# A streaming-encoder step on one core: the last four column groups of its input projection in two pairs, each by seven products in place of eight

## The chip, the core and the metric

The kernel runs on one core of one Trainium2 chip. A core has a matrix engine (TensorE, PE in the rows), a vector engine (VectorE, DVE), an activation engine (ScalarE, ACT), GpSimd (POOL) and SyncE (SP), which issues the DMAs. Each engine works through its own queue in order, and semaphores tie the queues together. The metric is the device time of one execution, in microseconds (us).

## The reference

Two layers of an encoder, for 512 new frames of one stream and 16 new frames of each of 8 running streams: 640 rows in all, in five tiles of 128 rows (the fifth is that of the running streams). All weights are shared by the five tiles. What matters here is the input projection, which feeds all three attention branches:

```python
h = _rms(x, p['norm_mix'])
(fq, fk, fv, fg, bq, bk, bv, iq, ik, iw, cqa, ckva, ckpe) = jnp.split(
    h @ p['w_in'], _split_points(IN_SPLITS), axis=-1)
fq = _rms(fq.reshape(B, T, FOX_HEADS, FOX_DIM), p['fox_gq'])   # likewise fk
bq = _rms(bq.reshape(B, T, DSA_HEADS, DSA_DIM), p['dsa_gq'])   # likewise bk, ik
...
g = jax.nn.sigmoid((h @ p['w_gate']).astype(f32)).astype(x.dtype)
x = x + (ga * ya + gb * yb + gc * yc) @ p['w_o']
h2 = _rms(x, p['norm_ffn'])
gt, up = jnp.split(h2 @ p['w_ffn_in'], 2, axis=-1)
x = x + (jax.nn.silu(gt) * up) @ p['w_ffn_out']
```

`h` is 640 x 1024 and `w_in` is 1024 x 2254, in float32.

## The kernel before

**The projection.** The 2254 columns of `w_in` are cut into six groups of 296 to 416 columns (`GROUPS`, L56). A group has four chunks: 256 of the 1024 rows of `w_in` (the contraction) by the group's columns, laid out as 128 partitions by twice the width. The stage with the chunks of group 2 to group 5 is what the change touches: 0 to 384 and 384 to 768 (queries and keys of branch A), 768 to 1158 (its values and gates), 1838 to 2254 (branch C). Groups 0 and 1 (branch B) stand ahead of them, and the gate projection (L872) behind them.

**Split products.** Each float32 operand is split into a high part and a rest, and a product is three matmuls: high by high, high by rest, rest by high. For every chunk ScalarE copies the raw weights into `w_hi` (`hi`, L1362; the instruction itself is L1358 in `copy`), and VectorE subtracts, `w_lo` = raw - `w_hi` (`lo`, L1855 to L1859). There are two buffers of each. `hi(c)` waits until the matmuls of chunk c-2 have ended (`w_used`), and the matmuls of chunk c wait for `lo(c)` (`lo_made`). `h` lies on the chip as `h_hi` and `h_lo`.

**TensorE.** `row_chunk` and `row_part` (L828 to L850): per chunk five tiles, two blocks of 128 contraction rows, three matmuls, so 30 matmuls of one column group's width. The tile of `h` is the stationary operand. Each tile has its own of the eight PSUM banks over the four chunks of a group; after the last chunk ScalarE copies the five results out (`p_d`, `p_i`, `p_qk`, `p_v`, `p_m`), and `proj_out` tells that a bank is free.

**VectorE beside it.** Between two splits `lo` it works on one tile of a branch: `dsa_sums` and `dsa_norm` for branch B in the chunks of groups 2 and 3, `fox_sums` and `fox_norm` for the queries and keys of branch A in groups 4 and 5. "Sums" squares the rows and adds them up per head (`sq_a`, `ssq`, L1927, L1939, L1933). GpSimd turns the sums into inverse roots (`rsq` = power -1/2, L1806), and "norm" multiplies the rows by them. All three queues are in program order: VectorE's is lo(c), norm(t-1), sums(t), lo(c+1), and so on.

**GpSimd.** Ahead of the inverse roots it fills three tiles with zeros (`wz`, `zi`, `lfr`), and beyond them it has nothing to do in this stage. In the feed-forward stage of the same layer it adds and subtracts blocks of weights (`w_sums`, L1829 to L1836), since that stage is already computed by a seven-product scheme.

**SyncE.** `chunk` (L558 to L562) loads each chunk of weights into one of two `raw` buffers, when `lo` has read the one before it.

## Time and profile before

| | us |
|---|---|
| median of three runs | 2193.6 (2193.42 to 2195.47) |
| the profiled execution, its time | 2195.58 |
| the profiled execution, its span | 2193.8 |
| TensorE busy in the span | 2133.1 (97%) |
| VectorE, ScalarE, GpSimd busy | 1378.5, 981.2, 389.4 |
| the four column groups, layer 0 | 59.1 to 145.3 |
| the four column groups, layer 1 | 1146.1 to 1232.3 |

The span is the time from the first to the last instruction of the profiled execution; 1.8 us of its time lie outside it. A busy share says how much of the span an engine worked, not that it set the end: for that the chain of waits is read, which follows the last instruction back to whatever released it. Matmuls overlap, so the duration in a matmul's row is longer than its share of the time; the distance between two starts, or a stretch divided by its matmuls, gives what one costs. The numbers of this table that are not in the page's head come from the start and end rows of the stage (the first two groups of rows below). In the rows below, times in a timeline are counted from the span's start. The two layers run the same instructions, 1087 us apart.

### The profile page before, as it was taken

What the parts mean: (1) busy time and instruction counts of PE and PEld (TensorE: products, weight loads), DVE (VectorE), ACT (ScalarE), POOL (GpSimd) and SP (SyncE); (2) the same over time, 40 slices, a digit from 0 to 9 for tenths busy, and PEclk for the clock granted to TensorE, in tenths of its full rate; (3) what the DMA queues carried; (4) which work ended last, traced back from release to release, by engine and by line L of the source; (5) the groups of instructions that cost most, each with busy time, mean ns of one, the idle gap of its engine ahead of it and who ended that gap; (6) DMA issues with size and microseconds to landing.
All of it is one profiled execution on the core that took longest, in us unless ns stands there. A gap on an engine that the chain in (4) does not pass through costs nothing.

```text
span 2193.8 us, 36974 instructions
## 1 busy us (share of the span) xinstructions
PE 2133.1 (97%) x13700; PEld 1887.9 (86%) x13700; DVE 1378.5 (63%) x2728; ACT 981.2 (45%) x2085; POOL 389.4 (18%) x282
## 2 busy tenths in 40 slices
PE   8999999999999999999999999899999999999999
PEld 7997768787988989989899877687889799899897
DVE  3466775545838937838445667655358488387493
ACT  4246666655525413314232466666563244143241
POOL 1120020200004414314011200203000043142230
PEclk9999999999999999999999999999999999999999
DMA  6233224123322222222232332231323222222222
GB/s 222 75 106 122 70 75 127 56 63 152 116 96 68 95 69 87 78 86 87 76 134 74 108 112 86 78 115 46 118 104 115 97 77 87 78 87 83 71 97 77
DMA packets 90929, 206.92 MB, mean 94 GB/s; under 512 B 20864, under 2 KB 47360, under 8 KB 90624
## 3 DMA queue, kind: packets, MB, share of 16 engines
q1 hardware_dynamic: 90752, 204.56, 28.2%
q8 instruction: 111, 1.82, 0.3%
q14 instruction: 66, 0.54, 0.1%
HBM read 180.58 MB, written 23.95 MB: 93 GB/s over the span
## 4 chain that ended last, share of the span: by engine, by line
PE 89%; DVE 3%; ACT 3%; issue 2%; POOL 1%; DVEq 1%; DMA 1%; SPq 0%; ACTq 0%
PE ps L832 27%; PE ps L872 15%; PE ps L1297 8%; PE ps L1298 8%; PE ps L1299 8%; PE ps L881 7%; PE ps L1022 2%; PE ps L1039 2%; PE ps L927 2%; PE ps L946 1%; PE ps L972 1%; POOL rsq L1806 1%; PE ps L1083 1%; DVEq L1852 1%; PE ps L1128 1%
## 5 line engine op out<-in xcount | busy, mean ns | idle before, releaser
L1358 ACT ACTIVATE w_hi<-raw 128x1024 fp32r<-128x1024 f32 (+4 forms) x172 | 171.1, 997 | 419.3 <-PE ps L832 369.6
L1859 DVE TENSOR_TENSOR w_lo<-raw,w_hi 128x1024 fp32r<-128x1024 f32 (+4 forms) x124 | 139.1, 1123 | 195.1 <-ACT w_hi L1358 191.4
L872 PE MATMUL ps<-h_hi,w_hi 128*128 128x320 f32 x768 | 248.7, 324 | 1.4 <-ACT g L1358 1.4
L872 PE MATMUL ps<-h_hi,w_lo 128*128 128x320 f32 x768 | 238.3, 310 | 0.0
L872 PE MATMUL ps<-h_lo,w_hi 128*128 128x320 f32 x768 | 238.2, 310 | 0.0
L1297 PE MATMUL ps<-th_hi,op_hi 128*128 128x320 f32 x640 | 199.2, 311 | 4.6 <-issue 4.6
L1806 POOL TENSOR_TENSOR rsq<-ssq,mhalf 128x12 f32<-128x12 f32 (+3 forms) x56 | 118.8, 2122 | 473.2 <-DVE ssq L1933 409.7
L1299 PE MATMUL ps<-th_hi,op_lo 128*128 128x320 f32 x640 | 199.0, 311 | 0.0
L1298 PE MATMUL ps<-th_lo,op_hi 128*128 128x320 f32 x640 | 199.0, 311 | 0.0
L832 PE MATMUL ps<-w_hi,act_hi 128*128 128x512 f32 x440 | 174.5, 397 | 0.0
L832 PE MATMUL ps<-w_lo,act_hi 128*128 128x512 f32 x440 | 174.4, 396 | 0.0
L832 PE MATMUL ps<-w_hi,act_lo 128*128 128x512 f32 x440 | 174.4, 396 | 0.0
L1358 ACT ACTIVATE op_hi<-w_sums 128x512 fp32r<-128x512 f32 x160 | 99.9, 631 | 146.8 <-PE ps L1299 116.9
L2281 DVE TENSOR_TENSOR w_lo<-raw,w_hi 128x1024 fp32r<-128x1024 f32 x48 | 59.8, 1249 | 158.3 <-ACT w_hi L1358 158.3
L872 PEld LDWEIGHTS ps<-h_hi,w_hi 128*128 128x128 f32 x768 | 145.5, 189 | 12.5 <-issue 10.4
L1298 PE MATMUL ps<-h_lo,op_hi 128*128 128x320 f32 x480 | 148.4, 309 | 0.0
L1297 PE MATMUL ps<-h_hi,op_hi 128*128 128x320 f32 x480 | 148.3, 309 | 0.0
L1299 PE MATMUL ps<-h_hi,op_lo 128*128 128x320 f32 x480 | 148.2, 309 | 0.0
L832 PE MATMUL ps<-w_hi,h_hi 128*128 128x384 f32 (+3 forms) x440 | 146.4, 333 | 0.3 <-DVE w_lo L1859 0.3
L872 PEld LDWEIGHTS ps<-h_lo,w_hi 128*128 128x128 f32 x768 | 145.7, 190 | 0.7 <-issue 0.3
L832 PE MATMUL ps<-w_lo,h_hi 128*128 128x384 f32 (+3 forms) x440 | 146.3, 332 | 0.0
L832 PE MATMUL ps<-w_hi,h_lo 128*128 128x384 f32 (+3 forms) x440 | 145.9, 332 | 0.0
(350 smaller groups left out, 5330.8 us busy)
## 6 DMA issues: line engine op xcount, KB each, us to landing
raw<-in_weights SPq DMA_DIRECT2D x212, 512.0 KB, 3.3
gates<-gst SPq DMA_DIRECT2D x72, 160.0 KB, 1.8
g<-gates SPq DMA_DIRECT2D x12, 960.0 KB, 7.3
raw<-in_weights SPq DMA_DIRECT2D x24, 384.0 KB, 3.0
ktb<-in_cache_fox_kt SPq DMA_DIRECT2D x16, 384.0 KB, 4.0
vc<-in_cache_fox_v SPq DMA_DIRECT2D x16, 384.0 KB, 3.3
x_sb<-in_x_prompt SPq DMA_DIRECT2D x8, 512.0 KB, 4.8
out_y_prompt<-x_sb SPq DMA_DIRECT2D x8, 512.0 KB, 3.4
```

The source lines that it names most:

```text
L832: mm = pe.matmul(ps[:, bank % 8, 0:width], x_pair[x][:, k0 + kk, t * P:(t + 1) * P], w[:, kk * width:(kk + 1) * width], start=first and kk ...
L872: mm = pe.matmul(ps[:, 5, 0:HALF], w[:, kk * P:(kk + 1) * P], h_pair[x][:, kk, half * HALF:(half + 1) * HALF], start=kk == 0 and n == 0, s ...
L881: mm = pe.matmul(ps[:, 2 * pair + half, 0:HALF], w[:, (w0 + kk) * P:(w0 + kk + 1) * P], x_pair[x][:, kk, half * HALF:(half + 1) * HALF], s ...
L927: last = pe.transpose(ps[0:cols, bank, n * P:n * P + rows], src, cst("ident", 0, rows, rows))
L1022: last = pe.transpose(ps[:, 3, j * P:j * P + rows], probs[0:rows, i % 3, j * P:(j + 1) * P], cst("ident", 0, rows, rows))
L1297: pe.matmul(ps[:, bank, 0:HALF], op_hi[i][:, a], x_hi, start=first and kk == 0, stop=False, skip_group_check=not first)
L1298: pe.matmul(ps[:, bank, 0:HALF], op_hi[i][:, a], x_lo, start=False, stop=False, skip_group_check=not first)
L1299: mm = pe.matmul(ps[:, bank, 0:HALF], op_lo[i][:, a], x_hi, start=False, stop=kk == 3, skip_group_check=not first)
L1358: return act.activation(dst, src, ACT.Copy, scale=scale)
L1806: pool.tensor_tensor(rsq[:, n % RSLOT, 0:width], ssq[:, n % RSLOT, 0:width], mhalf[:, 0:width], ALU.pow).then_inc(sq_root.sem, 1)
L1859: dve.tensor_tensor(low[:, 0:width], raw[raw_slot(c)][:, 0:width], high[:, 0:width].bitcast(F32), ALU.subtract).then_inc(lo_made.sem, 1)
L2281: dve.tensor_tensor(w_lo[c % 2][:, :], raw[raw_slot(c)][:, :], w_hi[c % 2][:, :].bitcast(F32), ALU.subtract).then_inc(lo_made.sem, 1)
```

## The change

The four groups form two pairs: pair 0 is 0 to 384 with 384 to 768; pair 1 is 1838 to 2254 with 768 to 1158, in a common width of 416. In each pair the two column groups (index 1, 2), the two halves of the contraction (512 rows each) and two pairs of tiles (tiles 0 and 1, tiles 2 and 3) form a two-by-two block product. In place of its eight block products seven are computed (P1 to P7), from sums and differences of blocks. The fifth tile is computed plainly, with the blocks B11, B21, B22 and B12 as they come by.

- **Steps.** A pair has 16 steps, one for each quarter of the contraction that an operand holds: P1, P2, P5, P6, P3, P7, B12, P4, each with m = 0 and 1. A P step has 12 matmuls for the tile pair (units u = 0 and 1), P1, P2 and P3 have 6 more for the fifth tile, and a B12 step has only these 6.
- **Weights.** The eight blocks of a pair lie in eight buffers `pw0` to `pw7` (`pair_raw`). P1 takes B11, P2 B21, P3 B22. For the others GpSimd first forms differences in place: P5 = B12-B11, then P6 = B22-(B12-B11), P4 = B21-P6, P7 = B22-B12.
- **Activations.** GpSimd forms four combinations of `h` (`s_full`) once a layer: four instructions put `h_hi` and `h_lo` together, four more add and subtract. ScalarE and VectorE split them (`s_hi`, `s_lo`).
- **Results.** The seven products are gathered in PSUM and, where that doesn't do, by VectorE additions of a bank to what ScalarE has copied out (`pair_added`, six in a pair).
- **Order.** VectorE's sums of tile t stand at step 2t+1 and its norm at step 2t+4. GpSimd's differences stand between the inverse roots. The three fills with zeros move behind the roots of branch A. The buffers `pw` of pair 1 are loaded one by one, when pair 0 has read them.

```diff
-GROUPS = [(1158, 384), (1542, 296), (0, 384), (384, 384), (768, 390), (1838, 416)]
+GROUPS = [(1158, 384), (1542, 296), (0, 384), (384, 384), (1838, 416), (768, 390)]
...
+PAIR_STEPS = [(_n, _m) for _n in ("P1", "P2", "P5", "P6", "P3", "P7", "B12", "P4") for _m in range(2)]
+PAIR_BANK = {"P1": 0, "P2": 1, "P5": 2, "P6": 0, "P3": 2, "P7": 0, "P4": 0}
+UNIT_BANKS = (((6, 3, 4), (5, 2, 7)), ((3, 4, 6), (2, 7, 5)))
+LAST_BANKS = (0, 1)
+SLOTS_OF = ({"B11": 0, "B21": 2, "B12": 4, "B22": 6}, {"B11": 6, "B21": 0, "B12": 4, "B22": 2})
...
+                UNIT_ROWS = {"P1": lambda u: tile_rows(0, u), "P2": lambda u: tile_rows(4, u), "P5": lambda u: sum_rows(0, u), "P6": lambda u: sum_rows(1, u),
+                             "P3": lambda u: sum_rows(3, u), "P7": lambda u: sum_rows(2, u), "P4": lambda u: tile_rows(4, u + 2)}
+                LAST_ROWS = {"P1": (0, 0), "P2": (4, 0), "P3": (4, 1), "B12": (0, 1)}
...
+                def pair_products(q):
+                    width = PAIR_WIDTH[q]
+                    for n, (name, m) in enumerate(PAIR_STEPS):
+                        c = pair_step(q, n)
+                        def product(rows, bank, first, last, alone):
+                            for kk in range(2):
+                                for i, (w, x) in enumerate(w_of(c)):
+                                    mm = pe.matmul(ps[:, bank, 0:width], rows(x, 2 * m + kk), w[:, kk * width:(kk + 1) * width],
+                                                   start=first and kk == 0 and i == 0, stop=last and kk == 1 and i == 2, skip_group_check=not alone)
+                            return mm
...
+                        pe.wait_ge(lo_made.sem, lo_made.at(L, MADE[c]))
+                        if m == 0 and name in ("P5", "P6", "P3", "P7"):
+                            pe.wait_ge(s_ready.sem, s_ready.at(L, {"P5": 1, "P7": 2, "P6": 3, "P3": 4}[name]))
+                        opens = name in ("P1", "P2", "P5")
+                        for u in range(2):
+                            if name != "B12":
+                                if m == 0:
+                                    bank_free(u)
+                                mm = product(UNIT_ROWS[name](u), UNIT_BANKS[q][u][PAIR_BANK[name]], opens and m == 0, m == 1, opens)
+                                if u == 0 and m == 1:
+                                    mm.then_inc(block_done.sem, 1)
+                            if u == 0 and name in LAST_ROWS:
+                                kk0, b = LAST_ROWS[name]
+                                if m == 0:
+                                    last_free()
+                                mm = product(tile_rows(kk0, TT - 1), LAST_BANKS[b], m == 0 and name in ("P1", "P3"), m == 1 and name in ("P2", "B12"), True)
+                                if (name, m) == ("P2", 1):
+                                    mm.then_inc(block_done.sem, 1)
+                        mm.then_inc(w_used.sem, 1)
...
+                def pair_hi(q, n):
+                    name, m = PAIR_STEPS[n]
+                    c, slot = pair_step(q, n), SLOTS_OF[q][BLOCK_OF[name]] + m
+                    if name in SUMMED:
+                        act.wait_ge(pair_sum.sem, pair_sum.at(L, 8 * q + SUMMED[name] + m + 1))
+                    else:
+                        act.wait_ge(pair_in[slot].sem, pair_in[slot].at(L, 16 * (q + 1)))
+                    act.wait_ge(w_used.sem, w_used.at(L, c - 1))
+                    copy(w_hi[c % 2][:, 0:2 * PAIR_WIDTH[q]], operand_of(q, n)).then_inc(hi_made.sem, 1)
...
+                        if q == 0 and n in (0, 1, 2):
+                            sum_hi(n + 1, (2, 1, 3)[n])
+                        if n == 1:
+                            pair_move(q, n, 1, 0, 0, 0)
...
+                def whole(dst, k0, a):
+                    rows = slice(k0, k0 + 4), slice(a, a + 2 * P)
+                    return pool.tensor_tensor(dst[:, :, :], h_hi[:, rows[0], rows[1]].bitcast(F32), h_lo[:, rows[0], rows[1]].bitcast(F32), ALU.add)
+                whole(s_full[2], 0, 2 * P)
+                whole(s_full[0], 4, 2 * P)
+                whole(s_full[1], 0, 0)
+                whole(s_full[3], 4, 0)
...
+                pool.tensor_tensor(s_full[0][:, :, :], s_full[2][:, :, :], s_full[0][:, :, :], ALU.add).then_inc(s_made.sem, 1)
...
+                    for name in names:
+                        for m in range(2):
+                            if name == "P5":
+                                landed("B12", m)
+                                split(m)
+                                dst, a, b = "B11", "B12", "B11"
+                            if name == "P6":
+                                landed("B22", m)
+                                split(4 + m)
+                                dst, a, b = "B11", "B22", "B11"
+                            if name == "P4":
+                                split(2 + m)
+                                dst, a, b = "B21", "B21", "B11"
+                            if name == "P7":
+                                split(6 + m)
+                                dst, a, b = "B11", "B22", "B12"
+                            pool.tensor_tensor(block(dst, m), block(a, m), block(b, m), ALU.subtract).then_inc(pair_sum.sem, 1)
+                        pool.drain()
...
                 for n, width in enumerate(ROOT_WIDTHS):
+                    for q in range(PAIRS):
+                        if n == TT * q + 1:
+                            pair_sums(q, ("P5",))
+                        if n == TT * q + 3:
+                            pair_sums(q, ("P6", "P4"))
+                        if n == TT * q + 4:
+                            pair_sums(q, ("P7",))
...
+                def pair_lo(q, n):
+                    c, w = pair_step(q, n), 2 * PAIR_WIDTH[q]
+                    dve.wait_ge(hi_made.sem, hi_made.at(L, c + 1))
+                    dve.tensor_tensor(w_lo[c % 2][:, 0:w], operand_of(q, n), w_hi[c % 2][:, 0:w].bitcast(F32), ALU.subtract).then_inc(lo_made.sem, 1)
...
+                for q, (sums, norm_rows) in enumerate(((dsa_sums, dsa_norm), (fox_sums, fox_norm))):
+                    for n in range(len(PAIR_STEPS)):
+                        pair_lo(q, n)
+                        if q == 0 and n == 0:
+                            dve.wait_ge(wq_in.sem, wq_in.at(L, 16 * 2))
+                        if q == 0 and n < 4:
+                            sum_lo(n, (0, 2, 1, 3)[n])
+                        if n == 5:
+                            pair_added(q, 3, 2, 1, 0, 0, 1)
+                        if n == 11:
+                            pair_added(q, 9, 6, 6, 1, 0, 2)
+                        if n == 13:
+                            pair_added(q, 11, 7, 4, 1, 1, 0)
+                        if n % 2 and n < 2 * TT:
+                            sums(n // 2)
+                        if n % 2 == 0 and 4 <= n < 2 * TT + 4:
+                            norm_rows(n // 2 - 2)
+                        if q == PAIRS - 1 and n == 14:```

On GpSimd, between the normalisation of `h` and the first roots of branch A, stood before (`rsq` are the inverse roots, with 6 values a row for branch B, 12 for branch A, 3 for branch C):

```order
L1772 MEMSET wz 128x1024 [waits ln_xn]
L1774 MEMSET zi 128x256
L1778 MEMSET lfr 128x510 [waits tab_saved]
L1806 TENSOR_TENSOR rsq<-ssq,mhalf 128x6 [waits sq_sum]
L1784 COPY v_dsa<-p_d 128x320 [waits proj_out]
L1806 TENSOR_TENSOR rsq<-ssq,mhalf 128x6 [waits sq_sum] x4
```

Now, from the first root to the last of branch B (the first two `pw` rows are P5, then P6, P4 and P7; `pair_in` tells that a block has landed):

```order
L2045 TENSOR_TENSOR rsq<-ssq,mhalf 128x6 [waits sq_sum]
L2000 TENSOR_TENSOR pw_78<-pw_82,pw_78 128x768 [waits lo_made,pair_in4]
L2000 TENSOR_TENSOR pw_79<-pw_83,pw_79 128x768 [waits lo_made,pair_in5]
L2023 COPY v_dsa<-p_d 128x320 [waits proj_out]
L2045 TENSOR_TENSOR rsq<-ssq,mhalf 128x6 [waits sq_sum] x2
L2000 TENSOR_TENSOR pw_78<-pw_84,pw_78 128x768 [waits lo_made,pair_in6]
L2000 TENSOR_TENSOR pw_79<-pw_85,pw_79 128x768 [waits lo_made,pair_in7]
L2000 TENSOR_TENSOR pw_80<-pw_80,pw_78 128x768 [waits lo_made]
L2000 TENSOR_TENSOR pw_81<-pw_81,pw_79 128x768 [waits lo_made]
L2045 TENSOR_TENSOR rsq<-ssq,mhalf 128x6 [waits sq_sum]
L2000 TENSOR_TENSOR pw_78<-pw_84,pw_82 128x768 [waits lo_made]
L2000 TENSOR_TENSOR pw_79<-pw_85,pw_83 128x768 [waits lo_made]
```

The fills have gone from the head, and eight differences stand between the five roots. The two of P6 stand behind the third root.

On VectorE, in the chunks of group 2, before (sums of tile 1, the next split, norm of tile 1):

```order
L1927 TENSOR_TENSOR sq_a_116<-p_d_113 128x320
L1927 TENSOR_TENSOR sq_a_116<-p_i_114 128x32
L1939 TENSOR_REDUCE ssq_70<-sq_a_116 128x5
L1939 TENSOR_REDUCE ssq_70<-sq_a_116 128x1
L1933 TENSOR_SCALAR ssq_70<-ssq_70 128x5
L1933 TENSOR_SCALAR ssq_70<-ssq_70 128x1
L1859 TENSOR_TENSOR w_lo1_60<-raw1_56,w_hi1_58 128x768 [waits hi_made]
L1927 TENSOR_TENSOR p_d_113<-p_d_113,rsq_71 128x256 [waits sq_root]
```

Now, from the split of step 5 (P5, m = 1) to that of step 6 (P6, m = 0), with the sums of tile 2 in between:

```order
L2266 TENSOR_TENSOR w_lo1_60<-pw1_79,w_hi1_58 128x768 [waits hi_made]
L2279 TENSOR_TENSOR p_qk_130<-p_qk_130,ps 128x384 [waits pair_out,block_done]
L2279 TENSOR_TENSOR p_qk_130<-p_qk_130,ps 128x384 [waits pair_out,w_used]
L2166 TENSOR_TENSOR sq_a_136<-p_d_133 128x320
L2166 TENSOR_TENSOR sq_a_136<-p_i_134 128x32
L2178 TENSOR_REDUCE ssq_70<-sq_a_136 128x5
L2178 TENSOR_REDUCE ssq_70<-sq_a_136 128x1
L2172 TENSOR_SCALAR ssq_70<-ssq_70 128x5
L2172 TENSOR_SCALAR ssq_70<-ssq_70 128x1
L2266 TENSOR_TENSOR w_lo0_59<-pw0_78,w_hi0_57 128x768 [waits hi_made]
```

Two additions have come between the split and the sums, and the sums of the third tile stand where the third root of GpSimd waits for them.

## Rows read from the trace of the kernel before

**Rows 1.** The page: shares of the chain that ended last, by engine.

```profile
PE 89%; DVE 3%; ACT 3%; issue 2%; POOL 1%; DVEq 1%; DMA 1%; SPq 0%; ACTq 0%
```

**Rows 2.** Busy time by engine in the two stretches of the four groups.

```profile
core 0: us, PE busy (x) PEld busy (x) DVE busy (x) ACT busy (x) POOL busy (x), PEclk, DMA share, GB/s
59.10:145.30 86.20, 86.03 (x482) 85.41 (x482) 47.63 (x118) 24.85 (x40) 20.47 (x11) 1.00 0.25 78
```

**Rows 3.** ScalarE's timeline: start, us, instruction, idle before it and releaser.

```profile
64.40 0.85 ACT L1358 ACTIVATE w_hi<-raw 128x768 fp32r<-128x768 f32 x1 [4.14 <-PE ps L832]
69.60 0.85 ACT L1358 ACTIVATE w_hi<-raw 128x768 fp32r<-128x768 f32 x1 [4.35 <-PE ps L832]
...
127.91 0.90 ACT L1358 ACTIVATE w_hi<-raw 128x832 fp32r<-128x832 f32 x1 [4.47 <-PE ps L832]
133.58 0.90 ACT L1358 ACTIVATE w_hi<-raw 128x832 fp32r<-128x832 f32 x1 [4.77 <-PE ps L832]
...
145.29 0.52 ACT L1358 ACTIVATE p_m<-ps 128x416 f32<-128x416 f32 x1 [0.62 <-PE ps L832]
```

**Rows 4.** VectorE's timeline: splits, sums and norms of both branches.

```profile
60.37 0.96 DVE L1859 TENSOR_TENSOR w_lo<-raw,w_hi 128x768 fp32r<-128x768 f32 x1 [3.46 <-ACT w_hi L1358]
61.24 0.49 DVE L1927 TENSOR_TENSOR sq_a<-p_d 128x320 f32<-128x320 f32 x1
...
61.91 0.58 DVE L1939 TENSOR_REDUCE ssq<-sq_a 128x5 f32<-128x320 f32 x2
...
76.55 0.42 DVE L1927 TENSOR_TENSOR p_d<-p_d,rsq 128x256 f32<-128x256 f32 x1
...
77.62 0.22 DVE L1974 COPY ikrep<-p_i 128x128 f32<-128x128 f32 x1
...
109.61 0.56 DVE L1927 TENSOR_TENSOR sq_a<-p_qk 128x384 f32<-128x384 f32 x1
...
112.41 0.97 DVE L1859 TENSOR_TENSOR w_lo<-raw,w_hi 128x780 fp32r<-128x780 f32 x1 [0.43 <-ACT w_hi L1358]
...
118.31 1.02 DVE L1859 TENSOR_TENSOR w_lo<-raw,w_hi 128x832 fp32r<-128x832 f32 x1
...
128.62 0.96 DVE L1927 TENSOR_TENSOR p_qk<-p_qk,rsq 128x768 f32<-128x768 f32 x1 [2.16 <-POOL rsq L1806]
129.66 0.56 DVE L1927 TENSOR_TENSOR p_qk<-p_qk,gains 128x384 f32<-128x384 f32 x1
```

**Rows 5.** GpSimd's timeline: the inverse roots.

```profile
62.87 1.33 POOL L1806 TENSOR_TENSOR rsq<-ssq,mhalf 128x6 f32<-128x6 f32 x1 [25.02 <-DVE ssq L1933]
...
112.06 2.27 POOL L1806 TENSOR_TENSOR rsq<-ssq,mhalf 128x12 f32<-128x12 f32 x1 [4.46 <-DVE ssq L1933]
118.49 2.97 POOL L1806 TENSOR_TENSOR rsq<-ssq,mhalf 128x12 f32<-128x12 f32 x1 [4.16 <-DVE ssq L1933]
```

**Rows 6.** GpSimd's groups by shape: count, busy, mean ns.

```profile
L1819 POOL TENSOR_TENSOR h_full<-h_hi,h_lo 128x512 f32<-128x512 f32 x4 | 5.1, 1288 | 4.2 <-DVE xn L1874 4.2
```

**Rows 7.** VectorE's groups by shape: an addition from PSUM, and a wide split.

```profile
L1859 DVE TENSOR_TENSOR w_lo<-raw,w_hi 128x1024 fp32r<-128x1024 f32 x80 | 98.0, 1225 | 101.7 <-ACT w_hi L1358 98.2
L2339 DVE TENSOR_TENSOR part<-part,ps 128x320 f32<-128x320 f32 x160 | 77.1, 482 | 21.3 <-PE ps L1299 19.2
```

**Rows 8.** GpSimd and VectorE in the feed-forward stage, one timeline each.

```profile
699.89 2.99 POOL L1829 TENSOR_TENSOR w_sums<-raw 128x512 f32<-128x512 f32 x1 [6.64 <-DVE op_lo L2276]
...
728.22 1.35 POOL L1833 TENSOR_TENSOR w_sums<-raw,raw 128x512 f32<-128x512 f32 x1 [0.16 <-issue]
...
728.34 1.78 DVE L2276 TENSOR_TENSOR op_lo<-raw,op_hi 128x512 fp32r<-128x512 f32 x1
...
730.44 0.68 DVE L2276 TENSOR_TENSOR op_lo<-w_sums,op_hi 128x512 fp32r<-128x512 f32 x1
```

**Rows 9.** Busy time in 2 us stretches around an idle TensorE, granted clock third from last.

```profile
410.00:412.00 2.00, 0.11 (x1) 0.14 (x2) 1.44 (x4) 2.00 (x5) 0.40 (x1) 1.00 0.23 82
...
414.00:416.00 2.00, 2.00 (x9) 2.00 (x9) 1.37 (x4) 1.55 (x5) 0.11 (x1) 0.50 0.00 0
```

247 lines of the change are left out of this document (192 added, 55 removed).

## The prediction

> **What bounds the kernel now.** I read the chain of waits first: TensorE has 89% of it, VectorE and ScalarE 3% each [rows 1]. A change pays where it shortens TensorE's work and keeps that work supplied. Then the stretch of the four column groups: in 86.2 us TensorE is busy for 86.03, at a granted clock of 1.00; VectorE for 47.63, ScalarE for 24.85, GpSimd for 20.47 [rows 2]. So this stage is bound by matmuls alone, and each split is ready in time. The price of a matmul comes from ScalarE's timeline, where each `w_hi` starts when a chunk of 30 matmuls has ended: 64.40 to 69.60 is 5.20 us, 173 ns for 384 columns; 127.91 to 133.58 is 5.67 us, 189 ns for 416 columns [rows 3].
>
> **What goes.** Per layer the two pairs had 2 x 240 matmuls. Now a pair has 14 P steps of 12 and 8 groups of 6 for the fifth tile, 216 matmuls. Pair 0: 216 x 173 ns = 37.4 us; pair 1, where every matmul is 416 wide: 216 x 189 ns = 40.8. Together 78.2 against 86.2, so 8.0 us a layer and 16 in all. That is what the change can give if TensorE never waits.
>
> **What feeding a step costs.** A chunk lasted 5.2 to 5.7 us and needed one split; a P step lasts 2.08 (12 x 173 ns) or 2.27 us, 3.1 or 3.4 with the fifth tile, and a B12 step 1.04 or 1.13. From the end of a step to the readiness of the one after next: ScalarE 0.85 or 0.90 [rows 3], VectorE 0.96 or 1.02 [rows 4], two handovers that I estimate at 0.05 each from the gap between a `w_hi`'s end and its `w_lo`: 1.9 to 2.0 us. In a 12-matmul step that just fits. In the B12 steps it does not: steps 13 and 14 each come about 0.9 late, 1.8 in pair 0 and, with 1.13 and wider splits, 2.0 in pair 1. These 3.8 us stand whatever else is true. The removed cover is the long chunk; nothing else hides a late split.
>
> **The chain into P6.** GpSimd's first P6 difference stands behind its third root, and that root waits for VectorE's sums of tile 2, which stand behind the split of step 5 and two additions. From the end of that split in pair 0:
> - two additions from PSUM, 0.48 for 320 columns [rows 7], taken as 0.50 from start to start: 1.0
> - sums of a branch B tile, from 61.24 [rows 4] to the root at 62.87 [rows 5]: 1.63
> - the root: 1.33 [rows 5]
> - the difference of 768 columns: GpSimd takes 1288 ns for 512 [rows 6], so 2.5 ns a column, 1.92, and 0.16 for the drain ahead of it (the idle time in [rows 8])
> - `w_hi` 0.85, `w_lo` 0.96, handovers 0.1; and about 1.0 more, since the second difference (next paragraph) is then running: 2.9
>
> Sum 8.9 us. Step 5 covers 2.08 of it, so TensorE stands still for 6.9 us. In pair 1 the sums are those of branch A, 109.61 to 112.06, 2.45 [rows 4, 5], the root 2.27 and the difference 2.08: 1.0 + 2.45 + 2.27 + 2.24 + 3.1 = 11.1, less 2.27, 8.8 us. Both: 15.7 us a layer, already twice the 8.0 saved.
>
> **Two engines at one port.** The rest comes from GpSimd's differences running beside VectorE. In the feed-forward stage a split of 512 columns takes 0.68 us alone, at 730.44; the one at 728.34, begun just after a GpSimd difference (728.22 to 729.57), takes 1.78 [rows 8]. It ends at 730.12, about the time of one split after the difference's end. The reverse is there too: the difference at 699.89 takes 2.99 in place of 1.28. A root on GpSimd does not hold VectorE up (the split at 112.41 takes its usual 0.97 beside the root from 112.06), but it waits at its start: 2.97 at 118.49, with a split from 118.31 [rows 4, 5]. Additions with one operand in PSUM keep their length. In the stage as it was there were no differences, so this is new there. The Trainium skill states it as a rule (SBUF — State Buffer, Who interferes with whom): a VectorE instruction with two SBUF inputs and a GpSimd instruction that reads SBUF exclude each other for their whole length. The trace agrees; without that rule the time would be that of rival B.
>
> VectorE's budget, pair 0: 16 splits at 0.90 from start to start, 14.4; four splits of the `h` combinations of 1024 columns at 1.2 [rows 7], 4.8; five tiles at 1.63 for the sums and 1.29 (76.55 to 77.84 [rows 4]) for the norm, 14.6; six additions, 3.0. That is 36.8 of its own work, against 37.4 of TensorE's. Eight differences of 1.92 are 15.4 us of held port; one falls in the P6 chain and some 4 us beside reductions and additions, which leaves 9.5. The idle time in the P6 chain is 1.33 + 2.1 + 0.95 = 4.4, that at the B12 and first steps some 2. Sum 52.7 us. Pair 1: splits 15.4, five tiles at 2.45 + 1.60 (128.62 to 130.22 [rows 4]) 20.3, additions 3.0, the gate bias 1.1: 39.8; held 16.6 - 2.1 - 5 = 9.5; idle in the P6 chain 5.5; and some 6 where differences are themselves held up by VectorE's runs, as at 699.89, so that P7's come late: 60.8. The two are 113.5 us where 86.2 stood: +27.3 a layer. TensorE's own account must come to the same: 78.2 of matmuls, 15.7 into P6, 3.8 at B12, and the remaining 15.8 spread over steps 3, 4, 7, 8 and 10 of both pairs.
>
> **The clock.** After TensorE had been nearly idle in 410 to 412 us, the granted clock of 414 to 416 was 0.50, the 1.2 GHz level, at 9 matmuls in 2 us [rows 9]. Standing still 7 to 9 us should do that here. Most of it is hidden, since the steps behind P6 wait for their splits anyway; I take +1.0 a layer, with 0 and 4 as its ends.
>
> **The other parts.** The eight instructions for the `h` combinations, 1024 columns each, 2.56 us by [rows 6], are 20.5 us of GpSimd from about 32 us on; the stage begins at 59.1, the splits of four earlier chunks may each be held for up to 2.6 us, and these chunks have about 2 us of slack: between 0 and 2.5 a layer, I take 0. The fills move behind work that is not waited for: 0. DMA: the same bytes in the stage; eight loads issued early, then one as each block is read, each needed several us later, so 0, though on SyncE's queue a late split now delays all loads behind it. The last roots end before the last steps, as before: 0.
>
> **Sum.** 27.3 + 1.0 = 28.3 a layer, 56.6 in all. Profiled execution 2195.6 + 56.6 = 2252.2; the median of the runs is 2.0 below it: 2250.
>
> **Rivals.**
> A, the work beside TensorE stays hidden and only the count of matmuls speaks: 2193.6 - 16.0 = 2177.6. For it speaks that VectorE had 38 us idle in the stage [rows 2]. Against it, the four waits in a row ahead of P6, of which none can overlap another. 5%.
> B, the P6 and B12 chains hold, but the port costs nothing: pair 0 45.4, pair 1 51.8, from the same schedule without the held time: 97.2, +11.0 a layer, 2216. Against it stand [rows 8]. 15%.
> C, as forecast, but every difference holds VectorE or is held by it in full, and the early chunks lose their 2.5 us: 6 + 4 + 2.5 more a layer, 2275. For it speaks the 2.99 us row; against it that many instructions on VectorE don't use the port. 12%.
> D, the matmul saving does not do what it says (216 for 240) or the two effects cancel, within 0.2% (4.4 us), which is about what a measurement tells from no change: 2%.
> The forecast's own case, 2236 to 2264: 66%.
> The other side of the forecast is A, and it decides where the P6 difference comes within 2.1 us of the split of step 5; the rows give 5.9 for it. Faster 5%, same 2%, slower 93%. The range from 2212 to 2275 leaves out A, D and part of C.
>
> **What would show it.** In the profile after: TensorE's matmuls fewer by 96; in each layer two idle stretches of 6 to 9 us ahead of the first P6 matmuls (`s_hi1`), ending on the split `w_lo`, whose chain leads over `w_hi`, the GpSimd difference and a root to the sums of VectorE; 1 us waits at step 13 and 14; splits of 768 columns of more than 0.96 us, up to 2.9; the two pairs 110 to 120 us long; and a granted clock of 0.5 in the first us behind P6's wait. It would be wrong if splits beside differences keep 0.96 us (then B), if the P6 idle stretch is under 3 us (then A), or if idle time appears behind the projection, which I price at nothing.

## The result, and the profile after

The changed kernel takes 2256.3 us (2252.0 to 2259.1, 4 runs), the kernel before beside it 2194.5 (2193.4 to 2197.0): a ratio of 1.0275, 95% interval 1.0262 to 1.0287. The forecast was 2250, with a range of 2212 to 2275. The profiled execution has a span of 2255.7 us.

The page after. TensorE's share of the chain fell from 89% to 84%, VectorE's and its queue's rose [rows 1]:

```profile
PE 84%; DVE 5%; ACT 3%; issue 3%; DVEq 2%; POOL 1%; DMA 1%; POOLq 1%; SPq 0%; ACTq 0%
```

TensorE has 13604 matmuls for 13700, the 96 fewer that were counted. The stage of the four groups, in each layer from the last move of `p_i` to the last of `p_m`, took 86.2 us and now takes 116.3 and 117.2. Both layers together that is 61.1 us, all but 0.6 of the difference of 61.7. The stretch in layer 0, columns as in [rows 2]:

```profile
core 0: us, PE busy (x) PEld busy (x) DVE busy (x) ACT busy (x) POOL busy (x), PEclk, DMA share, GB/s
60.11:176.39 116.28, 90.75 (x434) 84.27 (x433) 89.14 (x144) 41.03 (x58) 61.05 (x30) 0.90 0.11 34
```

VectorE is busy for 89.1 us where it was for 47.6, and the granted clock is 0.90. In this stage TensorE's marked waits (those that the timeline gives with a releaser) all end on one instruction, the split. For both layers: waited for in total us, times, and the longest.

```profile
PE ps L979 <- DVE w_lo L2266: 51.9, 28, 7.7
```

Four rows of layer 0 in TensorE's timeline, at P5, at both steps of P6, and at the second step of B12 (start, us, instruction, idle before and releaser):

```profile
75.49 0.44 PE L979 MATMUL ps<-w_hi,s_hi 128*128 128x384 f32 x1 [2.38 <-DVE w_lo L2266]
85.88 0.69 PE L979 MATMUL ps<-w_hi,s_hi 128*128 128x384 f32 x1 [5.76 <-DVE w_lo L2266]
91.33 0.69 PE L979 MATMUL ps<-w_hi,s_hi 128*128 128x384 f32 x1 [1.25 <-DVE w_lo L2266]
108.09 0.44 PE L979 MATMUL ps<-w_hi,h_hi 128*128 128x384 f32 x1 [0.93 <-DVE w_lo L2266]
```

In layer 1 the wait ahead of P6 is 4.38 us in pair 0. Pair 1 waits 7.74 us ahead of P6 in both layers. The chain into the wait of 5.76 us, VectorE first, then GpSimd and ScalarE, is the one that the prediction walks; its splits answer to those of [rows 4], its root to [rows 5]:

```profile
76.74 0.96 DVE L2266 TENSOR_TENSOR w_lo<-pw,w_hi 128x768 fp32r<-128x768 f32 x1
77.61 1.01 DVE L2279 TENSOR_TENSOR p_qk<-p_qk,ps 128x384 f32<-128x384 f32 x2
...
79.86 0.23 DVE L2172 TENSOR_SCALAR ssq<-ssq 128x5 f32<-128x5 f32 x2
...
84.16 1.67 DVE L2266 TENSOR_TENSOR w_lo<-pw,w_hi 128x768 fp32r<-128x768 f32 x1 [4.08 <-ACT w_hi L1481]
85.75 2.04 DVE L2166 TENSOR_TENSOR p_d<-p_d,rsq 128x256 f32<-128x256 f32 x1
87.71 1.84 DVE L2209 SCALAR_TENSOR_TENSOR p_d<-p_d,rsq,gains 128x64 f32<-128x64 f32 x1
```

```profile
80.16 1.32 POOL L2045 TENSOR_TENSOR rsq<-ssq,mhalf 128x6 f32<-128x6 f32 x1 [3.48 <-DVE ssq L2172]
81.45 3.56 POOL L2000 TENSOR_TENSOR pw<-pw,pw 128x768 f32<-128x768 f32 x2
85.17 4.31 POOL L2000 TENSOR_TENSOR pw<-pw,pw 128x768 f32<-128x768 f32 x2 [0.16 <-issue]
```

```profile
83.28 0.84 ACT L1481 ACTIVATE w_hi<-pw 128x768 fp32r<-128x768 f32 x1 [9.24 <-POOL pw L2000]
```

From the end of the split of step 5 (77.61) over additions, sums, root, first difference and `w_hi` to the matmul at 85.88 it is 8.3 us. The split of P6 takes 1.67 us beside the second difference, where the one at 76.74 takes 0.96. The next two products of VectorE, of 256 and of 64 columns, take 2.04 and 1.84 us beside the differences for P4: nearly the same for a fourth of the columns, since each waits for one instruction of GpSimd to end. Alone they take 0.42 and 0.27.

### The profile page after: what moved, and what is told of

The parts are those of the page before. It is cut to its first block, busy times and chain, and to the rows that moved or that the text cites. A ratio compares the mean times of both kernels' runs of the same rounds, so it can differ in the third digit from the quotient of the medians.

```text
span 2255.7 us, 37053 instructions
## 1 busy us (share of the span) xinstructions
PE 2143.8 (95%) x13604; PEld 1885.5 (84%) x13604; DVE 1473.5 (65%) x2792; ACT 1015.6 (45%) x2125; POOL 507.4 (22%) x330
## 4 chain that ended last, share of the span: by engine, by line
PE 84%; DVE 5%; ACT 3%; issue 3%; DVEq 2%; POOL 1%; DMA 1%; POOLq 1%; SPq 0%; ACTq 0%
PE ps L882 21%; PE ps L922 14%; PE ps L1420 7%; PE ps L1422 7%; PE ps L1421 7%; PE ps L931 6%; PE ps L979 3%; DVEq L2091 2%; PE ps L1144 2%; PE ps L1161 2%; PE ps L1049 1%; DVE w_lo L2266 1%; PE ps L1068 1%; PE ps L1094 1%; POOL rsq L2045 1%
## 5 line engine op out<-in xcount | busy, mean ns | idle before, releaser
L1481 ACT ACTIVATE w_hi<-raw 128x1024 fp32r<-128x1024 f32 (+2 forms) x140 | 143.6, 1029 | 319.5 <-PE ps L882 266.6
L2045 POOL TENSOR_TENSOR rsq<-ssq,mhalf 128x12 f32<-128x12 f32 (+3 forms) x56 | 124.6, 2225 | 408.9 <-DVE ssq L2172 341.6
L2098 DVE TENSOR_TENSOR w_lo<-raw,w_hi 128x1024 fp32r<-128x1024 f32 (+2 forms) x92 | 114.9, 1250 | 131.7 <-ACT w_hi L1481 128.2
L1481 ACT ACTIVATE op_hi<-w_sums 128x512 fp32r<-128x512 f32 x160 | 99.9, 631 | 150.7 <-PE ps L1422 120.8
L2068 POOL TENSOR_TENSOR w_sums<-raw 128x512 f32<-128x512 f32 x40 | 62.1, 1552 | 438.0 <-DMA raw<-in_weights 215.6
L922 PEld LDWEIGHTS ps<-h_hi,w_hi 128*128 128x128 f32 x768 | 144.8, 189 | 12.6 <-issue 10.1
L922 PEld LDWEIGHTS ps<-h_hi,w_lo 128*128 128x128 f32 x768 | 144.5, 188 | 0.0
L2553 DVE TENSOR_TENSOR op_lo<-w_sums,op_hi 128x512 fp32r<-128x512 f32 x160 | 121.4, 761 | 24.6 <-ACT op_hi L1481 18.0
```

The lines of the kernel that those rows point to most:

```text
L922: mm = pe.matmul(ps[:, 5, 0:HALF], w[:, kk * P:(kk + 1) * P], h_pair[x][:, kk, half * HALF:(half + 1) * HALF], start=kk == 0 and n == 0, s ...
L1481: return act.activation(dst, src, ACT.Copy, scale=scale)
L2045: pool.tensor_tensor(rsq[:, n % RSLOT, 0:width], ssq[:, n % RSLOT, 0:width], mhalf[:, 0:width], ALU.pow).then_inc(sq_root.sem, 1)
L2068: pool.tensor_tensor(w_sums[:, 0, :], up_first(c), up_second(c), ALU.add).then_inc(sums_made.sem, 1)
L2098: dve.tensor_tensor(low[:, 0:width], raw[raw_slot(c)][:, 0:width], high[:, 0:width].bitcast(F32), ALU.subtract).then_inc(lo_made.sem, 1)
L2553: dve.tensor_tensor(op_lo[i][:, :], operand_raw(c, i), op_hi[i][:, :].bitcast(F32), ALU.subtract).then_inc(lo_made.sem, 1)
```

## The experiments

The time of each is given with the ratio to the kernel before that ran beside it. "Stage" is the stretch of the four groups per layer, mean of both; the changed kernel's is 116.8 us, that of before 86.2.

### P6's differences ahead of the third root

```diff
-                        if n == TT * q + 3:
-                            pair_sums(q, ("P6", "P4"))
+                        if n == TT * q + 2:
+                            pair_sums(q, ("P6",))
+                        if n == TT * q + 3:
+                            pair_sums(q, ("P4",))
```

> The changed kernel with one move on GpSimd in both pairs: the two differences for the step P6 stand before the third tile's root instead of behind it. Theory A (VectorE and GpSimd share a port, so a difference that starts earlier only meets more of VectorE's work): the wait before P6 shrinks by 2 to 3 us per layer, about 2251 us. Theory B (only the length of the chain into P6 counts: the third tile's sums and root, some 4 to 5 us of it in each pair, leave it): 8 to 10 us per layer, about 2238 us.

Measured: 2242.7 us, 1.022 (1.0203 to 1.0237), stage 110.6, 6.2 us per layer less. It lies between the theories. The chain was shortened, but the port took part back. GpSimd's first P6 difference now meets the split of step 5, which takes 2.50 us, and the second one, which by the program waits for that split, starts only behind it:

```profile
75.34 1.82 POOL L2000 TENSOR_TENSOR pw<-pw,pw 128x768 f32<-128x768 f32 x1
78.12 1.85 POOL L2000 TENSOR_TENSOR pw<-pw,pw 128x768 f32<-128x768 f32 x1 [0.96 <-DVE w_lo L2268]
```

```profile
75.48 2.50 DVE L2268 TENSOR_TENSOR w_lo<-pw,w_hi 128x768 fp32r<-128x768 f32 x1
```

In pair 0 of layer 0 the one wait of 5.76 us became several of 0.3 to 1.7, and in pair 1 the wait before P6 fell from 7.74 to 4.21 us. VectorE's busy time in layer 0's stage rose from 89.1 to 95.0.

### The two additions behind the sums as well

```diff
-                        if n == 5:
-                            pair_added(q, 3, 2, 1, 0, 0, 1)
                         if n % 2 and n < 2 * TT:
                             sums(n // 2)
+                        if n == 5:
+                            pair_added(q, 3, 2, 1, 0, 0, 1)
```

> The same move, and on VectorE the two additions of the second block (about 1.0 us together) behind the third tile's sums, in both pairs. Theory A: a further 0 to 1 us per layer, 2249 to 2251 us, since the differences already run beside them and are held by whatever VectorE does next. Theory B: a further 1 us in each pair, 4 us in all, about 2234 us.

Measured: 2246.8 us, 1.023 (1.0214 to 1.0245); stage 111.6. The interval overlaps that of the version without this edit, the median is 4 us above it. There is no gain, so theory B falls here. The additions have one operand in PSUM, and in the version without this edit they run beside the second difference at their own length (77.90, 1.01 us for the two). With them gone from that place, the products of the sums stand there, and the second, of 32 columns, takes 1.83 us in place of 0.18:

```profile
80.13 1.83 DVE L2168 TENSOR_TENSOR sq_a<-p_i 128x32 f32<-128x32 f32 x1
```

### Fills in place of the differences

```diff
-                            pool.tensor_tensor(block(dst, m), block(a, m), block(b, m), ALU.subtract).then_inc(pair_sum.sem, 1)
+                            pool.memset(block(dst, m), 0.5)
+                            pool.drain()
+                            pool.memset(block(dst, m), 0.5)
+                            pool.drain()
+                            pool.memset(block(dst, m)[:, 0:400], 0.5).then_inc(pair_sum.sem, 1)
```

> Every difference on GpSimd is replaced by three fills of the same buffer with a constant (so the products of P5, P6, P4 and P7 are those of a constant): all waits, their order and about 1.6 to 2.0 us per difference on GpSimd stay, but nothing is read there. Theory A (port sharing is the largest term, priced at 15.8 us per layer in the prediction): VectorE's subtractions behind a difference are back at 0.4 to 1.2 us instead of 1.7 to 2.9, and the time falls by 30 to 36 us, to 2220 to 2226 us. Theory B (the chain's length): less than 4 us, above 2252 us, as the fills take as long as the differences alone.

Measured: 2224.9 us, 1.013 (1.0115 to 1.0146), 31 us below the changed kernel; stage 101.0, 15.7 us per layer less. The groups of VectorE in the whole execution, first the changed kernel, then this one (count, busy us, mean ns, idle before):

```profile
L2266 DVE TENSOR_TENSOR w_lo<-pw,w_hi 128x832 fp32r<-128x832 f32 x32 | 35.9, 1123 | 26.7 <-ACT w_hi L1481 25.8
L2266 DVE TENSOR_TENSOR w_lo<-pw,w_hi 128x768 fp32r<-128x768 f32 x32 | 35.7, 1115 | 23.0 <-ACT w_hi L1481 22.0 <-issue 0.2
```

```profile
L2270 DVE TENSOR_TENSOR w_lo<-pw,w_hi 128x832 fp32r<-128x832 f32 x32 | 32.8, 1024 | 28.4 <-ACT w_hi L1481 27.7
L2270 DVE TENSOR_TENSOR w_lo<-pw,w_hi 128x768 fp32r<-128x768 f32 x32 | 30.8, 962 | 25.3 <-ACT w_hi L1481 24.3 <-issue 0.2
```

The splits are back at their own length, but they gained only 8 us in both layers; most of the stretching had been in the normalisations (in layer 0's stage the squares take 7.1 us less than in the changed kernel, the norms' products 6.5, the splits of `pw` 3.1). In layer 0's stage VectorE is busy for 72.3 us in place of 89.1, at the same 144 instructions. GpSimd has as much to do as before and every wait is there; a fill and its drains last 2.2 us per difference, more than the 1.8 of a difference alone. So the 15.7 us are the price of reading at the same time, and not of GpSimd's time. The part of the clock in it was not separated: its mean in layer 0's stage went from 0.90 to 0.93.

### Fills, and P6's ahead of the third root

Both edits above.

> The changed kernel with both edits: fills in place of the differences (2224.9 us alone) and those for P6 ahead of the third root (2242.7 us alone, against 2256). Theory A (the chain into P6 is what is left once the port is free, waits of 5.4 us and more before P6): a further 5 to 8 us per layer, 2209 to 2215 us. Theory G (the early differences helped only because they met other work on the port): no further gain, 2222 to 2226 us.

Measured: 2204.2 us, 1.0028 (1.0018 to 1.0038); stage 90.6, 10.4 us per layer less than with fills alone, more than theory A's 5 to 8. The wait before P6 was a term of its own: with the port free, moving the two differences ahead of one root gives 10.4 us, with the port shared 6.2. Of the 10.4, 8.4 are marked waits (15.8 to 7.4 a layer, from TensorE's timeline), and most of the rest is matmuls that now run at the 2.4 GHz level.

### Matmuls that keep the clock up

```diff
+                        warm = {("P5", 0): 12, ("P6", 0): 24, ("P6", 1): 38, ("P7", 1): 11}.get((name, q), 0) if m == 0 else 0
+                        if warm:
+                            if name != "P5":
+                                pe.wait_ge(pair_add.sem, pair_add.at(L, 6 * q + 1))
+                            for _ in range(warm):
+                                pe.matmul(ps[:, UNIT_BANKS[q][0][2 if name == "P5" else 1], 0:width], h_hi[:, 0, 0:P], h_hi[:, 0, 0:width], start=True, stop=True)
```

> The changed kernel with matmuls whose results nobody reads in TensorE's longest waits of this stage: 12 before P5 of the first pair, 24 and 38 before P6, 11 before P7 of the second pair, in each layer. They are sized to end just before the wait does. Theory A (the clock's fall costs 1.0 us per layer, as the prediction has it, because the slower matmuls run while TensorE would wait for the next weights anyway): 2254 to 2256 us. Theory C (the slower matmuls behind each wait, 13.0 us per layer more than the same columns at full clock, are on the path): those behind the four filled waits come back, 10 to 20 us, 2236 to 2246 us.

Measured: 2261.3 us, 1.0293 (1.0278 to 1.0309), no gain; stage 117.0 against 116.8. Two microseconds behind the wait before P6, in the changed kernel and in this one (the clock is the third number from the end):

```profile
86.00:88.00 2.00, 2.00 (x7) 2.00 (x8) 2.00 (x2) 0.00 (x0) 2.00 (x2) 0.50 0.00 0
```

```profile
86.00:88.00 2.00, 1.19 (x7) 0.87 (x6) 2.00 (x2) 0.71 (x1) 2.00 (x2) 1.00 0.00 0
```

In the changed kernel the chip runs P6 at the 1.2 GHz level, after TensorE stood still for 5.76 us. Here it stays at 2.4 GHz, and the second wait grows from 1.25 to 3.10 us, so that P6's second step begins at the same distance from its first:

```profile
84.84 0.44 PE L979 MATMUL ps<-w_hi,s_hi 128*128 128x384 f32 x1 [1.66 <-DVE w_lo L2272]
...
90.29 0.45 PE L979 MATMUL ps<-w_hi,s_hi 128*128 128x384 f32 x1 [3.10 <-DVE w_lo L2272]
```

5.45 us in both. The 13.0 us of the expectation are not all the clock's. By the starts in TensorE's timeline, the changed kernel's stage is 12.7 us (layer 0) and 12.1 us (layer 1) longer than its 78.2 us of matmuls and its marked waits together; of that some 7 and 6 us are matmuls at the 1.2 GHz level, and the rest stands at the beginnings of steps, where some 4 us a layer are found at full clock too (see the version without differences). The idle matmuls brought the 7 and 6 down to 3 and 5, and the mean granted clock of the stage from 0.90 to 0.97 (layer 1: 0.91 to 0.96), and the stage stayed as long. So what was given back had been hidden; whether the rest is, this run does not show. Theory C falls, and theory A's 2254 to 2256 was not met either. Against the kernel before, 1.0293 and the changed kernel's 1.0275 have overlapping intervals, so the 5 us between them are not clear of noise. In the two profiles about 4 us more lie outside the stage, 2.3 of them a longer wait for the load of a cache (`vc`, 5.2 us in three waits for 2.9 in two); why it is longer was not followed up.

### No differences at all

```diff
-                    for name in names:
+                    for name in ():
...
-                    if name in SUMMED:
-                        act.wait_ge(pair_sum.sem, pair_sum.at(L, 8 * q + SUMMED[name] + m + 1))
-                    else:
+                    if True:
                         act.wait_ge(pair_in[slot].sem, pair_in[slot].at(L, 16 * (q + 1)))
...
-                        if name == "B11":
-                            sp.wait_ge(pair_sum.sem, pair_sum.at(L, SUMMED["P7"] + m + 1))
-                            own_wait(sp, sp_tick)
```

> No differences at all: ScalarE splits the raw blocks for P5, P6, P4 and P7 (so those products are of the wrong weights), and nothing waits for GpSimd's differences. Theory A (what is lost is port sharing, about 15.5 us per layer as the fills showed, and the chain into P6, about 12 us per layer of what was left): the stage takes 82 to 85 us per layer against 86.2 before, 2186 to 2196 us. Theory D (the shorter steps of four tiles are too short for VectorE's and ScalarE's own work, with or without differences): the stage stays above 92 us, 2206 us or more.

Measured: 2201.9 us, 1.0029 (1.0018 to 1.0039): slower than before, by a little. Stage 88.7. That is 4 us above theory A's upper end and 3 below theory D's lower one. In layer 0:

```profile
58.88:147.43 88.55, 82.11 (x434) 76.90 (x433) 70.60 (x144) 41.31 (x58) 26.59 (x14) 1.00 0.14 44
```

```profile
PE ps L976 <- DVE w_lo L2261: 12.6, 14, 1.7
```

Even with the differences for nothing the stage is 10.5 us longer than its 78.2 us of matmuls. The marked waits are 6.3 us of it per layer, 3.1 of them at B12 in layer 0 (0.93, 0.48, 1.19 and 0.47). The rest, some 4 us, are, by the starts in TensorE's timeline, other steps that begin up to 0.3 us late without a mark, about 0.1 us more from the first to the second matmul of a step that had to wait, and 0.5 us of matmuls at the lower clock.

### The same load in the kernel before

```diff
+                    if n % TT and n < 2 * TT:
+                        for _ in range(2):
+                            pool.tensor_tensor(spare[:, :, :], h_hi[:, 0:2, 0:384].bitcast(F32), h_lo[:, 0:2, 0:384].bitcast(F32), ALU.add)
+                            pool.drain()
...
```

> The kernel before, with 16 additions of 768 columns on GpSimd per layer, in pairs ahead of its roots in this stage, whose result nobody reads, and the three fills of zeros moved behind them. Same load on the port as in the changed kernel, but nothing waits for it save the roots. Theory A (the port costs time only where VectorE has no slack left in a step: 47.6 us of its work lie in 86.2 us here): VectorE's instructions are stretched to about 2 us beside the additions, and the time rises by 0 to 8 us, to 2195 to 2203 us. Theory E (the port's price is the same whatever stands around it, about 1 us per addition): 30 us, about 2225 us.

Measured: 2242.6 us, 1.022 (1.0205 to 1.0235), stage 108.9: 22.7 us per layer. My theory A failed, and so did theory E, which was too low: 1.4 us per addition. VectorE and GpSimd in step 81 us:

```profile
83.61 2.06 DVE L1933 TENSOR_TENSOR p_d<-p_d,rsq 128x256 f32<-128x256 f32 x1 [1.22 <-POOL rsq L1812]
85.59 1.85 DVE L1976 SCALAR_TENSOR_TENSOR p_d<-p_d,rsq,gains 128x64 f32<-128x64 f32 x1
...
89.67 0.95 DVE L1865 TENSOR_TENSOR w_lo<-raw,w_hi 128x768 fp32r<-128x768 f32 x1
```

```profile
81.61 1.97 POOL L1812 TENSOR_TENSOR rsq<-ssq,mhalf 128x6 f32<-128x6 f32 x1 [2.48 <-DVE ssq L1939]
83.56 3.81 POOL L1776 TENSOR_TENSOR spare<-h_hi,h_lo 128x768 f32<-128x768 f32 x2
```

What I had taken for slack was not: VectorE has 38.6 us without work in this stage [rows 2], but in branch A's steps with a normalisation its own run, with the 2.16 us that it waits for the root in it, is longer than the step. Two successive splits of branch A in the kernel before:

```profile
125.45 1.02 DVE L1859 TENSOR_TENSOR w_lo<-raw,w_hi 128x832 fp32r<-128x832 f32 x1
...
132.59 1.02 DVE L1859 TENSOR_TENSOR w_lo<-raw,w_hi 128x832 fp32r<-128x832 f32 x1
```

From one to the next it is 7.1 us, where the chunk of matmuls takes 5.67 [rows 3]; only the lead of the earlier steps hides it. With the load the same run takes 10.2 us (123.88 to 134.09), and that of branch B 8.2 (81.45 to 89.67) where the splits had come every 5.2 us with 1.1 to 1.7 us of idle time ahead of each. Both additions start as the norm starts; in branch B they are met by VectorE's short two-input instructions (256 and 64 columns), and each of these waits out nearly a whole addition.

### The same with fills

```diff
-                            pool.tensor_tensor(spare[:, :, :], h_hi[:, 0:2, 0:384].bitcast(F32), h_lo[:, 0:2, 0:384].bitcast(F32), ALU.add)
-                            pool.drain()
+                            for part in (slice(0, 768), slice(0, 768), slice(0, 400)):
+                                pool.memset(spare_flat[:, part], 0.5)
+                                pool.drain()
```

> The kernel before with GpSimd's 16 idle additions per layer (2242.6 us) replaced by three fills each of the same spare buffer: the same place and about 1.9 us of GpSimd's time each, but nothing is read. Theory A (the additions cost by the port alone): 0 to 6 us over before, 2195 to 2201 us. Theory F (they cost because the roots stand behind them on GpSimd and VectorE waits for the roots): most of the 47 us stays, above 2225 us.

Measured: 2195.6 us, 0.9994 (0.9985 to 1.0004): no change, stage 86.3. In place of the rows above:

```profile
83.66 0.43 DVE L1934 TENSOR_TENSOR p_d<-p_d,rsq 128x256 f32<-128x256 f32 x1 [1.53 <-POOL rsq L1813]
84.00 0.28 DVE L1977 SCALAR_TENSOR_TENSOR p_d<-p_d,rsq,gains 128x64 f32<-128x64 f32 x1
...
84.59 0.66 DVE L1980 COPY bkrep<-p_d 128x128 f32<-128x128 f32 x1
```

```profile
83.58 4.42 POOL L1777 MEMSET spare<- 128x768 f32 x6
```

GpSimd is as late with its roots, and TensorE doesn't notice. So the 47 us of the load come from its reading, which is the port's part, and not from its time. This also clears the fills as a substitute in the changed kernel.

### The combinations of h as fills

```diff
-                whole(s_full[2], 0, 2 * P)
...
-                pool.tensor_tensor(s_full[3][:, :, :], s_full[3][:, :, :], s_full[1][:, :, :], ALU.subtract).then_inc(s_made.sem, 1)
-                pool.drain()
+                for i, made in ((2, 0), (0, 0), (1, 0), (3, 0), (0, 1), (2, 1), (1, 1), (3, 1)):
+                    pool.memset(s_full[i][:, :, :], 0.25)
+                    pool.drain()
+                    last = pool.memset(s_full[i][:, :, :], 0.25)
+                    if made:
+                        last.then_inc(s_made.sem, 1)
+                    pool.drain()
```

> The changed kernel with GpSimd's eight combinations of the rows of h per layer replaced by two fills each (so the summed rows are constants and P5, P6, P7 and P3 are wrong), same buffers, same signals. Prediction: these combinations were priced at nothing, with 2.5 us per layer as the upper bound, because they run under the two plain groups whose steps have room: 2251 to 2256 us. Rival (the port's price holds there as in the idle load, 1.4 us for each instruction of 1.9 us): up to 10 us per layer, 2236 us.

Measured: 2255.7 us, 1.0268 (1.0251 to 1.0286), against 1.0275 for the changed kernel: nothing, as priced. They run from 33 us on, under steps with no sums and no norms. The port holds VectorE there too, but the splits have waited 2 to 7 us for ScalarE and have room behind them. The fourth split of the second plain group, in the changed kernel and in this one:

```profile
52.71 2.19 DVE L2098 TENSOR_TENSOR w_lo<-raw,w_hi 128x592 fp32r<-128x592 f32 x1 [3.26 <-ACT w_hi L1481]
```

```profile
51.68 0.78 DVE L2089 TENSOR_TENSOR w_lo<-raw,w_hi 128x592 fp32r<-128x592 f32 x1 [3.32 <-ACT w_hi L1481]
```

### The differences on VectorE

```diff
                         pair_lo(q, n)
+                        if n in (0, 1, 4, 5):
+                            pair_difference(q, "P5" if n < 2 else "P6", n % 2)
...
+                        if n == 6:
+                            pair_difference(q, "P4", 0)
+                            pair_difference(q, "P4", 1)
+                            dve.drain()
+                        if n in (7, 8):
+                            pair_difference(q, "P7", n - 7)
```

where `pair_difference` is the same subtraction on the vector engine, and GpSimd's `pair_sums` is gone.

> The changed kernel with the 16 differences per layer on VectorE, each right behind the split that frees its buffer (P5 at steps 0 and 1, P6 at 4 and 5, P4 at 6, P7 at 7 and 8 of each pair), and none on GpSimd. Nothing then shares the port, and the chain into P6 loses root, queue and 3.6 us of differences, at the price of 16 times 0.87 us more work on VectorE per layer. Theory A: VectorE has 72 us of its own work per layer in this stage without sharing, with the differences about 86, and becomes the bound: the stage takes 87 to 92 us, 2196 to 2206 us. Theory B (only the chain's length counts): the chain is 3 to 4 us shorter per pair, 7 us per layer, 2242 us.

Measured: 2220.9 us, 1.0124 (1.0107 to 1.0141), 35 us below the changed kernel; stage 98.4. The direction and most of the size are theory A's, but the stage is 6 us longer than its upper end, and the time 15 us: VectorE is busy for 84.2 of layer 0's 97.4 us, and its work is heaviest in the shortest steps, 4 to 7.

### The squares on ScalarE too

```diff
-                    mul(sq_a[:, 0:384], p_qk[:, t, 0:384], p_qk[:, t, 0:384])
-                    step(mul(sq_b[:, :], p_qk[:, t, 384:768], p_qk[:, t, 384:768]))
+                    dve.wait_ge(squared.sem, squared.at(L, TT + t + 1))
...
+                    for dst, src in parts:
+                        last = act.activation(dst, src, ACT.Square)
+                    last.then_inc(squared.sem, 1)
```

> The same, and the squares of the normalisation sums (two instructions per tile, 0.67 us for the first five tiles' set and 1.10 us for the second) on ScalarE instead of VectorE. Theory A: VectorE's work falls by 9 us per layer to about 77 us, under the 78.2 us of matmuls, and the stage takes 82 to 86 us, 2185 to 2194 us: as before or a little faster. Theory D (steps too short for the chain of split, difference and split): no better than 92 us, 2206 us or more.

Measured: 2212.7 us, 1.0083 (1.0068 to 1.0098); stage 94.0: theory D holds here, not A. VectorE's work fell to 76.5 us as planned, but in steps 4 to 7 (8.3 us of matmuls) stand two norms, two sums, both additions and five differences beside the four splits, which are 13 us by the lengths above; hence the next one.

### Work spread over the steps

```diff
+SUMS_AT = ((2, 3, 6, 10, 12), (1, 2, 3, 6, 9))
+NORM_AT = ((9, 11, 13, 14, 15), (3, 7, 10, 12, 14))
...
```

P4's differences move to steps 7 and 8, P7's to 8 and 9, and the two copies of keys per tile to GpSimd.

> The version with differences on VectorE and squares on ScalarE (2212.7 us), rearranged so that each step's VectorE work fits its matmuls as far as it goes: the sums at steps 2, 3, 6, 10, 12 and 1, 2, 3, 6, 9, the normalisations at 9, 11, 13, 14, 15 and 3, 7, 10, 12, 14, P4's differences at 7 and 8, P7's at 8 and 9, and the two copies of keys per tile on GpSimd (they read one buffer each). Theory A (VectorE's work, about 74.5 us per layer, still has to fit beside 32 splits that come when ScalarE has them): stage 88 to 91 us per layer, 2199 to 2205 us, no faster than before. Rival (only its unevenness was the limit): stage under 85 us, 2190 us or less, faster than before.

Measured: 2201.4 us, 1.0017 (1.0008 to 1.0026), stage 88.4 (layer 0 89.2, layer 1 87.7), as theory A has it. In 59.0 to 149.4 us:

```profile
59.00:149.40 90.40, 84.60 (x443) 79.82 (x442) 75.44 (x130) 47.79 (x80) 29.52 (x24) 0.98 0.15 47
```

This is the best form of the scheme that I found. It takes back 55 of the 62 us, and is still not faster than the kernel before.

## Why the prediction was right

**The matmuls.** 8.0 us fewer per layer was right by the count of 96. What is gained by it can be seen only where nothing waits, and no version got there.

**The port.** Priced at 15.8 us per layer in TensorE's account; taking it away gives 15.7 (116.8 to 101.0). That the two numbers agree so closely is luck: the working reached its term as a remainder. The mechanism is shown by the pair of loads in the kernel before: about the same time on GpSimd with reading (+47 us) and without (no change). Here the rule of the Trainium skill (SBUF — State Buffer, Who interferes with whom) is borne out in three parts. VectorE with two SBUF inputs excludes a GpSimd instruction that reads SBUF: 0.27 became 1.84 us. It does not exclude one that only writes: 0.28 beside a fill. A copy, which the page says can take both port pairs, does meet fills: the copy of keys takes 0.66 beside them against 0.23 otherwise. For one instruction the page's rule goes too far, and the measurement decides: a root reads SBUF as well, and VectorE's split beside it keeps its 0.97 us [rows 4, 5].

**The chain into P6.** From the end of the split of step 5 to the first P6 matmul 8.9 us were forecast, 8.3 came; in pair 1 11.1 and 10.4 (131.7 to 142.15). Additions, sums and root came as forecast; the first difference took 1.8 us instead of 2.1, and from it over `w_hi` and the held split to the matmul it was 2.6 instead of 2.9. The waits were 6.9 and 8.8 by the forecast, 5.76 and 7.74 in layer 0, 4.38 and 7.74 in layer 1: 15.7 against 13.5 and 12.1. Taking sums and root out of it, with a free port, gives 10.4 per layer: most of the term is what stands in front of the difference, not the difference.

**B12.** Priced 3.8 per layer, marked waits 2.8 (0.93, 0.47, 0.97, 0.45 in layer 0). Right in place, a little high: the first wait of each pair came at the 0.9 us forecast, the second is half of it.

**The clock.** +1.0 per layer. It fell to 0.50 by the end of each wait before P6 or within a microsecond behind it, as forecast. No price on the path was found: with the mean clock up from 0.90 to 0.97 the stage is 117.0 us, and 116.8 without.

**The h combinations.** 0, right.

**The sum.** 28.3 per layer forecast, 30.6 measured. Rival B, the same schedule with a free port, was 97.2 us and measured 101.0, so 3.8 us were missing there. The port came out at 15.7 where the forecast's stage (113.5) lies 16.3 above B's, and the clock at nothing for 1.0: that gives 1.6 of the 3.8 back. In the version with fills, the waits at P6 and B12, priced at 19.5, are 15.7; the term that had no price is what stands beside the matmuls and the marked waits, some 7 us a layer, by the starts in TensorE's timeline half of it matmuls at the lower clock and half late starts of ordinary steps. So two errors of opposite sign met.

The same holds for VectorE's budget, which gave 113.5 us. It is 76.6 of own work, 19.0 of held time (9.5 in each pair) and 17.9 of idle time. In layer 0 VectorE is busy for 70.6 us where there are no differences, 18.5 more in the changed kernel, and idle for 27.1. The held time was right, the own work 6 us too high and the idle time 9 too low. The prediction's two accounts also price the port differently, 25.0 us on VectorE (held time and 6 for late differences) and 15.8 on TensorE, and the second is the one to compare with 15.7.

Rival A fails even in the version without any differences: that is 88.7 us, not 78.2. The rule by which it would have decided, P6 in reach of step 5, was too kind: without any difference 14 of 64 steps still began with a marked wait for a split.

The steps show it in one table (us per layer, mean of both layers):

| stage | us | step |
|---|---|---|
| changed kernel | 116.8 | |
| differences as fills, nothing read | 101.0 | -15.7 port |
| and P6 ahead of the root | 90.6 | -10.4 chain into P6 |
| no differences at all | 88.7 | -2.0 what is left of their chain |
| matmuls alone | 78.2 | -10.5: 6.3 marked waits for splits, some 4 of late starts |
| kernel before | 86.2 | |

## What to carry to other kernels

Fewer matmuls can be worth nothing where each product needs its own operand made by other engines: divide the saving by the number of new steps (here 8.0 us over 32) and compare it with one late start. Before putting two-input work on GpSimd, look for VectorE's short two-input instructions beside it, since here each paid for nearly a whole GpSimd instruction; the busy share of VectorE doesn't show it, the run of its work between two waits does. A lower clock behind a wait can be a mere symptom, as it was here; fill the wait with idle matmuls once, and see whether the time moves, before counting it as a cause.

## What I had not expected of the hardware

- VectorE's busy share does not foretell the port's price: 16 additions cost 22.7 us per layer in a stage in which VectorE worked for 47.6 of 86.2 us, and the eight combinations of `h`, which stretch splits from 0.78 to 2.19 us in front of it, cost nothing.
- Keeping the clock at 2.4 GHz through a wait of 6 us changed nothing in the stage.
- A fill on GpSimd stretches VectorE's copies of 128 columns from 0.23 to 0.66 us, and leaves its two-input products at 0.28.
- At the 2.4 GHz level the first matmul behind a wait takes 0.28 to 0.30 us until the second starts, where 0.17 to 0.19 is usual; at the 1.2 GHz level it is 0.48 to 0.52, where 0.32 to 0.35 is usual.
